# Gated products of three token tiles and the sample moved from ahead of the first expert tile into its stream of slots

## The chip, the cores and the metric

The program runs on one core of a Trainium2 chip (trn2). The metric is the device time of one execution in microseconds. A core has five engines that run their own instruction lists and meet at semaphores: TensorE (PE in the profile, its weight loads PEld), VectorE (DVE), ScalarE (ACT), GpSimd (POOL) and SyncE (SP); 16 DMA engines move data between memory (HBM), the on-chip buffer (here one tensor, `arena`, 53200 floats on each of 128 partitions) and itself. SP, ACT and POOL issue transfers.

## The reference

One step of a two-layer trunk, in float32, for a prompt of 512 tokens and a sample of 8 rows, with width 1024. Layer 0 is a state-space mixer, then an expert layer; layer 1 is latent attention, then an expert layer; every part has a modulated norm before it and a gated sum after it. The parts that the change touches:

```python
y = jnp.real(jnp.einsum("blgn,gpn->blgp", h, c_mat)) + d_skip * uf      # state-space output
z = jax.nn.gelu(y.reshape(bsz, length, D_MODEL))
a, g = jnp.split(z @ w_glu, 2, axis=-1)                                  # w_glu: 1024 x 2048
out = a * jax.nn.sigmoid(g)                                              # the gated product
x = x + ga1 * out
h = modulate(rmsnorm(x, g_norm[layer, 1]), sh2, sc2)
# experts: q = h @ w_q (1024 x 2048), scores against 2 x 128 keys for each of 8 heads,
# the best 16 of 16 x 16 candidates of each head, g = softmax of their scores; then for each of
# the 128 chosen experts of a token:  act = gelu(h . u[idx]);  y += g * act * v[idx]
x = x + ga2 * peer(h, w_q, sub_keys, u_emb, v_emb)
```

## The kernel before

**The gated product** (TensorE from L2080, ScalarE from L1062, VectorE from L1556, SP from L690). When the last round `y` of the state products is copied out, ScalarE applies the gelu in five instructions (four quarters j of the prompt and the sample) to `z5`. Here "j" isn't a run of 128 tokens: a chunk holds eight tokens, 2 halves of 4, and j is the place in the half, so the result has to go through memory (`x1_dram`) to come back as tiles of 128 consecutive tokens. For each j TensorE turns the 8 blocks (L2089), ScalarE copies them (L1069), and then come four units: unit q is the product with one quarter of the columns of `w_glu`, arranged so that a unit holds 256 columns of a and the 256 of g that belong to them, 8 matmuls of 128x512 (L2101). Two banks of PSUM alternate. ScalarE makes the sigmoid of g (L1077), VectorE multiplies (L1562), and after four units multiplies by the gate of the modulation and adds the residual row (L1568). SP stores each j (L704), waits for all stores, and only then issues the loads of the expert layer: modulation rows, the first two tiles (L744), and the query weights in four quarters (L730) and the keys.

**The expert layer** works on tiles t of 128 tokens (0 to 3 in layer 0; tile 4 is the sample). What each engine does in which order is written out by `peer_plan`: a list of steps that every engine goes through, doing the steps that are its own. The preparation of a tile is: squares, means, roots, norm, shifted (a modulated norm), turn, turned, then four query quarters m of four pieces each (`query`, L2132, eight 128x128 matmuls a piece), with a copy (L1107), a score product (`score`, L2145) and its copy (L1116) after each. Then for each of 8 heads six steps `top` (VectorE's search for the best 16, which writes the head's 16 row numbers) and shift, exps, gates (the softmax). The stream of a tile is 128 slots. In slot m GpSimd gathers one row of u and v for each token (L938, 1 MiB in one indirect DMA) into one of six ring buffers; VectorE makes the dot (L1688); ScalarE a gelu, a product with the gate and a diagonal of 32x32 blocks (L1146, L1158, L1161); TensorE adds the weighted v to the sum in PSUM (L2185, eight matmuls on 32x32 blocks). GpSimd reuses a ring buffer after TensorE's sum. The preparation of tile t+1 is spread over the slots of tile t by the lists `extra[slot]`; for tile 0 it stands ahead of the first slot as far as its first head, and heads 1 to 7 are done in slots 1 to 45, six steps a head.

Sigmoid, exp, sqrt and gelu need different tables in ScalarE, so a change between them shows as ACT_TABLE_LOAD.

Of the kernel before, what the change touches and what calls it, by code (L numbers as in the profile page):

```python
# [11 lines left out]
ALU = mybir.AluOpType  # L12
# [3 lines left out]
P = 128  # L16
# [4 lines left out]
NB = 8  # L21
# [37 lines left out]
def program(nc, a):  # L59

    with ExitStack() as ctx:
# [84 lines left out]
        z5 = at(SJ, (TC // 2) * D).rearrange("p (j d) -> p j d", j=TC // 2)  # L146
# [71 lines left out]
        s_x1 = sem("mixer_out_ready")  # L218
        s_out = sem("outputs_stored")
# [7 lines left out]
        LATE_GLU, LATE_Q, LATE_HEADS = 16, (48, 128), 96  # L227
# [7 lines left out]
        def row_no(passes, stage, j):  # L235

            slot = row_slot(stage, j)
            before = sum(row_slot(q, m) == slot for q in passes[:passes.index(stage)] for m in range(5))
            return 16 * (before + sum(row_slot(stage, m) == slot for m in range(j + 1)))
# [33 lines left out]
        zt = [at(U2 + i * D, D).rearrange("p (k t) -> p k t", k=KD) for i in range(2)]  # L273
        gate = [at(U2 + 2 * D + i * 256, 256) for i in range(2)]
        glu_t = [at(U2 + 2 * D + 512 + i * D, D) for i in range(2)]
        QW = KD * MB
        wglu_at = [at(MINB, QW)] + [at(CL + q * QW, QW) for q in range(3)]
# [33 lines left out]

        def rows_of(t):
            return P if t % 5 < 4 else NB
# [24 lines left out]
        s_pmr = sem("peer_mods_ready")  # L338
# [37 lines left out]
        def peer_plan(layer):  # L376
# [26 lines left out]
            for steps in first[:21]:  # L403
                plan += steps
            plan += [("top", t0, 0, part) for part in range(6)]
            plan += [("shift", t0, 0, 1), ("exps", t0, 0, 1), ("gates", t0, 0, 1)]
            for b in range(5):
                t = t0 + b
                extra = [[] for _ in range(slots_of(t))]
                if b == 0:  # L410
                    for m, steps in enumerate(first[21:36]):
                        extra[m // 3] += steps
                    for h in range(1, PH):
                        for part in range(6):
                            extra[6 * h + part - 5].append(("top", t0, h, part))
                        extra[6 * h].append(("shift", t0, h, h + 1))
                        extra[6 * h + 1].append(("exps", t0, h, h + 1))
                        extra[6 * h + 2].append(("gates", t0, h, h + 1))
# [31 lines left out]
        EXPS = [step for plan in PLAN for step in plan if step[0] == "exps"]  # L450

        def exp_no(t, h0):

            return [step[1:3] for step in EXPS].index((t, h0)) + 1

# [161 lines left out]
        def _(sp):  # L617
# [65 lines left out]
            sp.dma_start(wglu_at[0], a["w_glu"][:, 0:QW]).then_inc(s_wglu, 16)  # L683
# [6 lines left out]
            wait_copied(sp, ("y", NR - 1))  # L690
            sp.wait_ge(s_wglu, 16)
            for q in range(1, 4):
                sp.dma_start(wglu_at[q], a["w_glu"][:, QW * q:QW * (q + 1)]).then_inc(s_lw if q == 1 else s_wglu, 16)
            sp.wait_ge(s_out, 32)
            for s in range(2):
                sp.dma_start(at(BL, 4 * D, 64 * s, 64 * s + 64), x5v[s]).then_inc(s_x5, 16)
            sp.dma_start(at(BL + 4 * D, D, 0, NB), a["x_sample"]).then_inc(s_x5, 16)
            sp.dma_start(at(BL + 5 * D, D, 0, NB), mod_dram[1:NC9, 2 * D:3 * D]).then_inc(s_x5, 16)
            sp.dma_start(mod_a, mod_dram[0:1, 2 * D:3 * D].partition_broadcast(P)).then_inc(s_x5, 16)
            x1v = x1_dram.rearrange("(c s j) d -> s j c d", s=2, j=TC // 2)  # L700
            for j in range(TC // 2):
                sp.wait_ge(s_x1, j + 1)
                for s in range(2):
# [1843 lines left out]
```

## Time and profile before

| | us |
|---|---|
| median of 3 runs (lowest, highest) | 3956.45 (3954.03, 3964.04) |
| the profiled execution | 3956.18 |
| its span, first to last instruction | 3954.4 |
| mean granted TensorE clock in it | 0.761 of full speed |

| engine | busy us in the span | share |
|---|---|---|
| PE | 2770.6 | 70% |
| DVE | 2377.8 | 60% |
| ACT | 1232.7 | 31% |
| POOL | 1197.0 | 30% |

The page cuts the span into 40 slices of 98.9 us. Each digit is the share of the slice in which the engine was busy, in tenths, and 9 means 90% or more. Line numbers (L2101) are those of the kernel. In a group of instructions "out<-in" names the tensors, the shape stands as partitions x elements, and a float32 matmul leaves two records, so that a unit of eight matmuls is x16. In brackets stands the idle time of the engine before the instruction and what ended it.

### The profile page before, as it was taken

The numbers are of one execution on the slowest core, as the hardware profiler recorded it, in microseconds if no ns is written. First come the engines' busy times: TensorE is split into PE (matmuls) and PEld (weight loads), VectorE is DVE, ScalarE is ACT, GpSimd is POOL, SyncE is SP. The second block draws the span as 40 slices with busy tenths as digits, with TensorE's granted clock in tenths as the row PEclk, the third lists the DMA queues.
The fourth block names the chain that finished last, engine by engine and source line by source line (L and its number), as shares of the span: only waits on it lengthen the run. The fifth ranks groups of instructions, "written<-read, shape, count | busy, mean of one in ns | idle before, by whom it ended". The sixth has DMA issues, their size and how long they took to land.

```text
span 3954.4 us, 63127 instructions
## 1 busy us (share of the span) xinstructions
PE 2770.6 (70%) x24972; PEld 1044.8 (26%) x24972; DVE 2377.8 (60%) x5650; ACT 1232.7 (31%) x3821; POOL 1197.0 (30%) x1089
## 2 busy tenths in 40 slices
PE   4565877776866866656677899677768668766665
PEld 2354333320400410100043566442204003100100
DVE  8544018787677677554522344277886766775645
ACT  1212004433333333323321222134343334334333
POOL 5200003344444444433300001033444444443432
PEclk7767987777967866757788899777768677776767
DMA  8764238999999999999920203479999999999997
GB/s 325 182 190 134 78 139 323 387 409 420 409 420 420 415 416 419 418 405 419 381 67 6 94 17 150 161 306 392 407 420 401 420 420 412 412 420 401 417 421 329
DMA packets 208878, 1263.84 MB, mean 320 GB/s; under 512 B 54488, under 2 KB 55392, under 8 KB 62520
## 3 DMA queue, kind: packets, MB, share of 16 engines
q0 software_dynamic: 151552, 1109.46, 68.6%
q1 hardware_dynamic: 56480, 150.09, 11.2%
q8 instruction: 181, 2.97, 0.3%
q10 hardware_dynamic: 576, 0.59, 0.0%
q14 instruction: 89, 0.73, 0.0%
HBM read 1247.58 MB, written 10.12 MB: 318 GB/s over the span
## 4 chain that ended last, share of the span: by engine, by line
DMA 40%; PE 32%; DVE 17%; ACT 5%; issue 4%; SPq 1%; DVEq 1%; POOL 0%; ACTq 0%; PEldq 0%; POOLq 0%
DMA arena<-peer_uv,arena 35%; PE psum L2185 9%; DVE arena L1688 8%; PE psum L2132 6%; PE psum L2101 3%; DMA arena<-b_mod 2%; PE psum L2460 2%; PE psum L2263 2%; PE psum L2236 1%; DVE arena L1599 1%; ACT arena L1161 1%; ACT arena L1158 1%; ACT arena L1146 1%; PE psum L2324 1%; DVE arena L1351 1%
## 5 line engine op out<-in xcount | busy, mean ns | idle before, releaser
L2185 PE MATMUL psum<-arena 32*32 32x512 f32 x16384 | 1583.2, 848 | 813.9 <-ACT arena L1161 810.0
L1688 DVE SCALAR_TENSOR_TENSOR arena<-arena 128x1024 f32<-128x1024 f32 x1040 | 1274.8, 1226 | 784.7 <-DMA arena<-peer_uv,arena 773.8
L938 POOL DMA_INDIRECT arena<-peer_uv,arena x1040 | 1095.1, 1053 | 2148.8 <-PE psum L2185 1525.4
L2185 PEld LDWEIGHTS psum<-arena 32*32 32x32 f32 x16384 | 219.2, 121 | 2065.7 <-ACT arena L1161 2015.5
L1146 ACT ACTIVATE arena<-arena 128x1 f32<-128x1 f32 x1040 | 210.5, 202 | 1561.0 <-DVE arena L1688 1560.4
L1161 ACT ACTIVATE arena<-arena 128x32 f32<-128x32 f32 x1024 | 329.0, 321 | 33.4
L1158 ACT ACTIVATE arena<-arena 128x1 f32<-128x1 f32 x1040 | 306.0, 294 | 33.8
L2132 PE MATMUL psum<-arena 128*128 128x128 f32 x2048 | 269.3, 289 | 7.3 <-DMA arena<-peer_wq 6.2
L2132 PEld LDWEIGHTS psum<-arena 128*128 128x128 f32 x2048 | 251.4, 201 | 80.7 <-issue 79.2
L1342 DVE TENSOR_TENSOR arena<-arena 128x512 f32<-128x512 f32 (+6 forms) x187 | 156.0, 834 | 95.2 <-ACT arena L1252 76.8
L2020 PE MATMUL psum<-arena 128*9 128x128 f32 x2048 | 100.4, 377 | 111.3 <-DMA arena<-b_mod 111.3
L2101 PE MATMUL psum<-arena 128*128 128x512 f32 (+1 forms) x320 | 142.7, 607 | 17.1 <-DVE arena L1562 10.7
L2020 PEld LDWEIGHTS psum<-arena 128*9 128x9 f32 x2048 | 71.5, 122 | 138.8 <-issue 100.0
L1562 DVE TENSOR_TENSOR arena<-psum,arena 128x256 f32<-128x256 f32 (+1 forms) x20 | 8.4, 422 | 148.7 <-ACT arena L1077 116.9
L1351 DVE SCALAR_TENSOR_TENSOR arena<-arena 128x1024 f32<-128x1024 f32 (+3 forms) x61 | 70.9, 1163 | 40.7 <-DMA arena<-mod_rows 22.0
L1010 ACT ACTIVATE arena<-psum 9x128 f32<-9x128 f32 x128 | 34.5, 269 | 193.5 <-PE psum L2025 191.1
L970 POOL DMA_INDIRECT arena<-cache_kv,arena x8 | 7.5, 942 | 267.6 <-PE psum L2346 206.1
L1599 DVE MAX8 arena<-arena 128x8 f32<-128x128 f32 (+1 forms) x204 | 61.9, 331 | 43.9 <-ACT arena L1116 41.5
L1688 DVE DVE_READ_ACCUMULATOR arena<-arena 128x1 f32 x1040 | 85.5, 82 | 0.0
L2101 PEld LDWEIGHTS psum<-arena 128*128 128x128 f32 (+1 forms) x320 | 55.3, 175 | 101.5 <-issue 93.8
L1883 DVE TENSOR_REDUCE arena<-psum 128x1 f32<-128x128 f32 (+3 forms) x64 | 31.4, 490 | 84.2 <-PE psum L2327 83.8
L2460 PE MATMUL psum<-arena 128*128 128x512 f32 (+1 forms) x160 | 77.7, 648 | 4.8 <-ACT arena L1312 4.8
(262 smaller groups left out, 2503.8 us busy)
## 6 DMA issues: line engine op xcount, KB each, us to landing
arena<-w_mod SPq DMA_DIRECT2D x64, 1024.0 KB
arena<-peer_uv,arena POOLq DMA_INDIRECT x1040, 10.4
arena<-peer_wq SPq DMA_DIRECT2D x8, 2048.0 KB, 16.7
arena<-w_glu SPq DMA_DIRECT2D x4, 2048.0 KB, 12.4
arena<-x_prompt SPq DMA_DIRECT2D x4, 1024.0 KB
arena<-x_after_layer SPq DMA_DIRECT2D x8, 512.0 KB
arena<-w_o SPq DMA_DIRECT2D x1, 4096.0 KB
arena<-mod_rows SPq DMA_DIRECT2D x2, 1536.0 KB
```

Of the source, the lines that this page charges most:

```text
L938: pool.indirect_dma_start(ring[r], None, a[f"peer_uv{t // 5}"], bass.IndirectOffsetOnAxis(ap=ix, axis=0)).then_inc(landed[r], 16)
L1146: act.activation(col, col, ACT.Gelu_apprx_tanh).then_inc(s_gl, 1)
L1158: act.activation(wcol, col, ACT.Copy, scale=gate_).then_inc(s_gl, 1)
L1161: act.activation(diag[:, n_ % RING, :], eye32, ACT.Copy, scale=wcol).then_inc(s_dg, 1)
L1342: link(dve.tensor_tensor(out, x, y, op))
L1351: link(dve.scalar_tensor_tensor(out=out, in0=x, scalar=s, in1=y, op0=op0, op1=op1))
L1688: dve.scalar_tensor_tensor(out=u, in0=u, scalar=1.0, in1=h, op0=ALU.mult, op1=ALU.mult, accum_out=at(DOTS + (t % 2) * 2 * P + m, 1)).then_ ...
L2020: ins = pe.matmul(mod_bank(b, q), silu[:, k, :], w[k // 4][:, k % 4, MQ4 * q:MQ4 * (q + 1)], start=(k == 0), stop=False, skip_group_check= ...
L2101: ins = pe.matmul(psum[0:rows, 4 + m % 2, :], zt[j % 2][:, k, 0:rows], wglu[:, k, :], start=(k == 0), stop=(k == KD - 1))
L2132: ins = pe.matmul(psum[:, 4 + m % 2, P * q:P * q + R], wq[:, m, k, P * q:P * (q + 1)], htr[:, k, 0:R], start=(k == 0), stop=(k == KD - 1))
L2185: ins = pe.matmul(acc_of(t, i, c), diag[rows, r, :], ring[r][rows, D + 512 * c:D + 512 * (c + 1)], start=(m == 0), stop=last, skip_group_c ...
L2460: ins = pe.matmul(psum[0:R, 6 + n_, :], ot[:, k, 0:R], wo[:, k, 512 * n_:512 * (n_ + 1)], start=(k == 0), stop=(k == KD - 1))
```

## The change

Tokens are now taken in runs of 128: the copy of the turned blocks puts them in order of tokens (`ztv`), so that the residual row is a plain tile of `x_prompt`, and the sum stays where the expert layer reads it. All 32 turns of the prompt are done at once, the gelus go by rounds, and only the four units of tokens 0 to 127 stand ahead of the expert layer. The 12 units of tokens 128 to 511 and one unit of the sample (four products side by side in four column strips) are steps `glu` of the plan in slots 4 to 55 of tile 0, a quarter of a unit in each, with `gate` (sigmoid) one slot and `gsum` (VectorE's three steps on 256 columns) two slots after a unit's last quarter. To give the weights of the gated product a place, the query weights of tile 0 are loaded into the ring buffers and one more place (`WQ0`), and loaded again into their own place as the quarters of `w_glu` are done with (`glu_beside_experts`); quarter 0 of `w_glu` is loaded twice too. GpSimd's first six gathers therefore wait for query products. Two more query quarters stand ahead of the first slot (`ahead = 26`), the heads 2 to 7 of tile 0 are spread over slots 7 to 60, tile 1's preparation begins at slot 58 instead of 40, and two of its heads are searched in its own stream. Only tiles 2 and 3 and the sample are stored to `x1_dram`.

```diff
             first = [[] for _ in range(64)]
             prep(t0, first, 0)
-            for steps in first[:21]:
+            ahead = 21 if layer else 26
+            for steps in first[:ahead]:
                 plan += steps
...
                         for part in range(6):
-                            extra[6 * h + part - 5].append(("top", t0, h, part))
-                        extra[6 * h].append(("shift", t0, h, h + 1))
...
+                            m = 6 * (h - 1) + part
+                            m = 1 + m if layer or m < 6 else 7 + int(1.5 * (m - 6))
+                            extra[m].append(("top", t0, h, part))
...
+                    if layer == 0:
+                        for u in range(4, len(UNITS)):
+                            m = 4 * (u - 3)
+                            for piece in range(4):
+                                extra[m + piece].append(("glu", u, piece))
+                            extra[m + 4].append(("gate", u))
+                            extra[m + 5].append(("gsum", u))
+                        extra[100].append(("smods",))
+                if t == 1:
+                    for m in range(12):
+                        extra[1 + int(1.3 * m)].append(("top", t, 6 + m // 6, m % 6))
...
-                    at_ = 40 if b == 0 else 10
+                    at_ = 58 if t == 0 else 40 if b == 0 else 10
                     prep(t + 1, extra, at_)
                     at_ += 22 if b < 3 else 30
-                    gap = 1.3 if b == 0 else 1.5 if b == 3 else 1.75
-                    heads = heads_of(t + 1)
+                    gap = 1.25 if t == 0 else 1.3 if b == 0 else 1.5 if b == 3 else 1.75
+                    heads = 6 if t == 0 else heads_of(t + 1)
...
+            sp.wait_ge(s_mm, len(ROUNDS))
+            for q in (1, 2):
+                sp.dma_start(at(WGLU[q], QW), a["w_glu"][:, QW * q:QW * (q + 1)]
+                             ).then_inc(s_lw if q == 1 else s_wglu, 16)
+            sp.dma_start(at(X1[0], D), a["x_prompt"][0:P]).then_inc(s_x5, 16)
...
+            sp.dma_start(at(WGLU[3], QW), a["w_glu"][:, QW * 3:QW * 4]).then_inc(s_wglu, 16)
+            sp.wait_ge(s_out, 32)
+            sp.dma_start(at(KEYS, 2 * PH * P), a["peer_keys"][0]).then_inc(s_pw, 16)
+            for m in range(4):
+                if m == 0:
+                    sp.wait_ge(s_zt, 4)
+                if m == 1:
+                    sp.wait_ge(s_gm, 2)
+                sp.dma_start(at(WQ0[m], QW), a["peer_wq"][0][:, QW * m:QW * (m + 1)]
+                             ).then_inc(s_lw if m else s_pw, 16)
...
+            sp.wait_ge(s_pq, 4)
+            sp.dma_start(at(WGLU[0], QW), a["w_glu"][:, 0:QW]).then_inc(s_wglu, 16)
+
+            def glu_beside_experts():
+
+                for m, q in enumerate((1, 2, 3, 0)):
+                    sp.wait_ge(s_gm, units_done(q))
+                    peer_weights(0, m)
...
+                for j in (2, 3):
+                    sp.wait_ge(s_x1, x1_no(j))
+                    sp.dma_start(x1_dram[P * j:P * (j + 1)], at(X1[j], D)).then_inc(s_out, 16)
...
                 if n_ >= RING:
                     pool.wait_ge(freed[r], n_ // RING)
+                else:
+                    pool.wait_ge(s_pq, n_ // 2 + 1)
...
+            for r in range(NR):
+                wait_copied(act, ("y", r))
+                act.activation(z5[:, :, RG * GP * r:RG * GP * (r + 1)].rearrange("p j (g q) -> p j g q", g=RG),
+                               h5[:, RG * r:RG * (r + 1)].rearrange("p g j q -> p j g q"), ACT.Gelu_apprx_tanh
+                               ).then_inc(s_gelu, 1)
...
+            def glu_gate(u):
+
+                act.wait_ge(s_gm, u + 1)
+                if u >= 2:
+                    act.wait_ge(s_ga, u - 1)
+                act.activation(gate[u % 2], psum[:, unit_bank(u), 256:512], ACT.Sigmoid).then_inc(s_sg, 1)
...
+                if t == 1:
+                    dve.wait_ge(s_out, 32 + 48)
...
+                n_ = KD // pieces
+                for k in range(n_ * piece, n_ * (piece + 1)):
+                    if j == 4:
+                        for c in range(4):
+                            ins = pe.matmul(psum[32 * c:32 * c + NB, unit_bank(u), :], zts[:, k, :],
+                                            wide(WGLU[c])[:, k, :], start=(k == 0), stop=(k == KD - 1))
+                    else:
+                        w = wide(WGLU0 if u == 0 else WGLU[q])
+                        ins = pe.matmul(psum[:, unit_bank(u), :], ztk[:, k, P * j:P * (j + 1)], w[:, k, :],
+                                        start=(k == 0), stop=(k == KD - 1))
```

## Rows read from the trace of the kernel before

**Rows 1.** The page's slices, 98.9 us each: GB/s moved by the DMA engines.

```profile
GB/s 325 182 190 134 78 139 323 387 409 420 409 420 420 415 416 419 418 405 419 381 67 6 94 17 150 161 306 392 407 420 401 420 420 412 412 420 401 417 421 329
```

**Rows 2.** Stretches: length, busy us and instructions of each engine, clock, DMA share, GB/s.

```profile
395.00:410.00 15.00, 15.00 (x32) 6.23 (x31) 0.00 (x0) 1.22 (x2) 0.00 (x0) 0.90 1.03 355
...
421.00:555.00 134.00, 130.21 (x320) 52.08 (x320) 17.19 (x26) 9.88 (x22) 0.00 (x0) 0.98 0.07 16
...
640.00:744.00 104.00, 64.96 (x640) 9.13 (x640) 98.56 (x302) 53.35 (x144) 39.15 (x38) 0.66 0.99 395
744.00:832.00 88.00, 75.58 (x832) 42.74 (x824) 58.97 (x155) 31.24 (x105) 36.85 (x34) 0.90 0.99 391
```

**Rows 3.** Waits from 380 to 613 us: total us, times, longest.

```profile
ACT arena L1077 <- PE psum L2101: 146.8, 20, 19.6
```

**Rows 4.** Instructions in order of time, gated products to first gather: start, us.

```profile
394.59 15.74 PE L2101 MATMUL psum<-arena 128*128 128x512 f32 x32 [2.80 <-ACT arena L1069]
...
410.37 0.38 ACT L1077 ACTIVATE arena<-psum 128x256 f32<-128x256 f32 x1 [6.48 <-PE psum L2101]
...
421.02 16.16 PE L2101 MATMUL psum<-arena 128*128 128x512 f32 x32 [10.70 <-DVE arena L1562]
...
430.77 0.42 DVE L1562 TENSOR_TENSOR arena<-psum,arena 128x256 f32<-128x256 f32 x1 [9.56 <-ACT arena L1077]
...
498.61 27.73 PE L2101 MATMUL psum<-arena 128*128 128x512 f32 x64 [1.11 <-ACT arena L1069]
...
558.26 0.28 SPq L706 DMA_DIRECT2D xs_after_mixer<-arena  x1
...
570.50 1.03 ACT L1085 ACTIVATE psum<-arena 128x1024 f32<-128x1024 f32 x1 [15.21 <-DMA arena<-x_after_mixer]
...
584.16 13.39 PE L2132 MATMUL psum<-arena 128*128 128x128 f32 x96 [6.20 <-DMA arena<-peer_wq]
...
608.04 1.11 POOL L938 DMA_INDIRECT arena<-peer_uv,arena  x1 [437.86 <-DVE arena L1654]
```

**Rows 5.** Instructions in order of time, in the stream of slots.

```profile
613.67 1.23 DVE L1688 SCALAR_TENSOR_TENSOR arena<-arena 128x1024 f32<-128x1024 f32 x1 [4.66 <-DMA arena<-peer_uv,arena]
...
636.40 1.28 ACT L1138 ACT_TABLE_LOAD   x1
...
637.93 1.28 ACT L1146 ACT_TABLE_LOAD   x1
...
639.48 1.23 DVE L1688 SCALAR_TENSOR_TENSOR arena<-arena 128x1024 f32<-128x1024 f32 x1
...
655.72 1.22 DVE L1688 SCALAR_TENSOR_TENSOR arena<-arena 128x1024 f32<-128x1024 f32 x1
...
770.42 2.05 PE L2132 MATMUL psum<-arena 128*128 128x128 f32 x16
772.40 1.09 PE L2185 MATMUL psum<-arena 32*32 32x512 f32 x16
...
784.17 2.05 PE L2132 MATMUL psum<-arena 128*128 128x128 f32 x16
...
952.24 1.23 DVE L1688 SCALAR_TENSOR_TENSOR arena<-arena 128x1024 f32<-128x1024 f32 x1 [1.25 <-DMA arena<-peer_uv,arena]
...
1661.82 1.05 PE L2153 MATMUL psum<-arena 128*8 128x512 f32 x8
```

**Rows 6.** Fourth tile beside loads: gather landings 640 to 744, then 1697 to 1750.

```profile
DMA to landing us min/median/max: 7.5/9.0/10.5
...
DMA to landing us min/median/max: 15.4/20.7/27.3
...
L1688 DVE SCALAR_TENSOR_TENSOR arena<-arena x25: 1224/1226/1227, 1684.6 to 1772.0; 128x1024 f32<-128x1024 f32 x25
...
1691.73 1.96 PE L2185 MATMUL psum<-arena 32*32 32x512 f32 x16 [1.39 <-ACT arena L1161]
...
arena<-w_uq SPq DMA_DIRECT2D x1, 3072.0 KB
```

More of the change, by code:

```diff
@@ L237, in row_no @@
             slot = row_slot(stage, j)
-            before = sum(row_slot(q, m) == slot for q in passes[:passes.index(stage)] for m in range(5))
-            return 16 * (before + sum(row_slot(stage, m) == slot for m in range(j + 1)))
+            mine = [(q, m) for q in passes[:passes.index(stage) + 1] for m in range(5 if q != stage else j + 1)
+                    if row_slot(q, m) == slot and not (passes is LOADS and q == "peer0" and m < 2)]
+            return 16 * len(mine)
         ROUNDS = ([("u", r) for r in range(NR)] + [("k", r) for r in range(NR)]
@@ L410, in peer_plan @@
                 if b == 0:
-                    for m, steps in enumerate(first[21:36]):
+                    for m, steps in enumerate(first[ahead:36]):
                         extra[m // 3] += steps
@@ L1202, in peer_act @@
                         final_roots(*which)
+                    elif what == "gate":
+                        glu_gate(*which)
             def input_squares(j):
@@ new lines, in peer_mods, with glu_sum @@
+            def peer_mods(layer, rows, gain):
+                sc = at(PMOD + (D if rows == P else 4 * D), D, 0, rows)
+                return dve.scalar_tensor_tensor(out=sc, in0=sc, scalar=1.0, in1=at(gain, D, 0, rows), op0=ALU.add,
+                                                op1=ALU.mult)
+            dve.wait_ge(s_pmod, 32)
+            link(peer_mods(0, P, PTMP))
+            dve.wait_ge(s_x5, 48 + 32)
+            def glu_sum(u):
+                j, q = UNITS[u]
+                if u == 4:
+                    dve.wait_ge(s_x1r, 16 * 5)
+                dve.wait_ge(s_sg, u + 1)
+                quarters = range(4) if j == 4 else (q,)
+                for c in quarters:
+                    rows = slice(0, P) if j < 4 else slice(32 * c, 32 * c + NB)
+                    y = glut if j < 4 else at(GLUT, 256, 0, NB)
+                    ga = at((GA if j < 4 else GAS) + 256 * c, 256, 0, P if j < 4 else NB)
+                    x = at(X1[j] + 256 * c, 256) if j < 4 else at(X1S + 256 * c, 256, 0, NB)
+                    ins = dve.tensor_tensor(y, psum[rows, unit_bank(u), 0:256], gate[u % 2][rows], ALU.mult)
+                    if c == quarters[-1]:
+                        ins.then_inc(s_ga, 1)
+                        dve.wait_ge(s_ga, u + 1)
+                    else:
+                        link(ins)
+                    tt(y, y, ga, ALU.mult)
+                    ins = dve.tensor_tensor(x, x, y, ALU.add)
+                    if c == quarters[-1] and (j == 4 or (j, q) == [unit for unit in UNITS if unit[0] == j][-1]):
+                        ins.then_inc(s_x1, 1)
+                        dve.wait_ge(s_x1, x1_no(j))
+                    else:
+                        link(ins)
@@ L1572, in peer_means, with sample_mods @@
+            for u in range(4):
+                glu_sum(u)
+            def sample_mods():
+                dve.wait_ge(s_pmod, 80)
+                link(peer_mods(0, NB, HSP))
             def peer_means(t):
@@ L2200, in peer_pe @@
                         peer_turn(*which)
+                    elif what == "glu":
+                        glu_piece(*which)
                     elif what == "query":
```

241 lines of the change are left out of this document (130 added, 111 removed).

## The prediction

> **What bounds the kernel now.** I read the page's slices first: 78 and 139 GB/s are moved in the fifth and sixth slice (395 to 593 us), and 387 to 420 from the eighth on, up to the attention part [rows 1]. The table of stretches says why: from 421 to 555 us TensorE is busy 130 of 134 us at nearly full clock while 16 GB/s move; from 640 us on the transfers hold 391 to 395 GB/s at a share of 0.99 and TensorE has idle time in most of it [rows 2]. The first is the gated product, 20 units of eight 128x512 products (4 tiles and the sample times 4 weight quarters). The second is the expert stream: each slot gathers 1 MiB (1.049 MB, 2.50 us at the 420 GB/s of the fuller slices), VectorE forms a dot, ScalarE a weight, TensorE a weighted sum. The waits ahead of the stream say the same: ScalarE waits 146.8 us for the products of L2101, once for each of 20 units [rows 3]. What is done there for tiles 1 to 3 and the sample isn't needed by the first expert tile, and GpSimd issues nothing until 608.04 us [rows 4].
>
> The stream of the first tile isn't purely DMA-bound. Its 128 slots run from 613.67 to 952.24 us, 338.6 us or 2.65 each [rows 5]. In slots 8 to 47 VectorE is full: six slots take 16.24 us (2.71 each), which hold six dots and one head's search [rows 5], and it is busy 98.56 of 104 us [rows 2]. In the stretch with the next tile's queries TensorE sets the pace: a query piece of 2.05 and a sum of 1.09, overlapping a little, in four slots of five; five slots take 13.75 us, 2.75 each [rows 5].
>
> **The start of the stream, step by step.** (a) Today the first product starts at 394.59 us [rows 4]. After the change the gelus go round by round beside the state products, so only the last is left behind them, but all 32 turns and four copies come before the first product. Today one gelu of the five, eight turns and one copy lie there, after one gelu of four everything else is ready; I estimate +0.9 us, within -1 and +4. (b) Four units remain: the first two as now, 15.74 us, two more at 6.87 (four take 27.73) = 13.7, then gate 0.38 and three 256-wide VectorE steps of 0.42 with gaps, 1.9 [rows 4]. They end at 426.9 us. The stall of 10.70 us in front of the third unit [rows 4], where VectorE waits for the last row load, goes: the four units have a bank each and the gate row is loaded earlier. Late next are the weights: the third unit needs 8 MiB (8.4 MB) that start at 386 us, 24 us at the 355 GB/s of that stretch today [rows 2], 410 against the unit's 411; it is hidden with nothing to spare, which is most of the +4. (c) The way through memory, from 558.26 (store) to 570.50 (squares), 12.24 us, goes, since the row is left in the tile. (d) From the squares to the first gather is 37.54 us; in it TensorE idles 6.20 us until 584.16 for query weights, of which a copy of the turned rows needs about 1.1 (the squares over as many elements took 1.03) [rows 4]. Those weights are now issued beside the units (11 MiB, 32 us at 355 GB/s, by 418 us), so 32.5 stay. The order ahead of the stream holds one or two more query quarters, but they run beside VectorE's search and delay only what no one waits for; GpSimd's new wait for a query count in its first six gathers is met before each is due. First gather: 394.59+0.9+31.4+32.5 = 459.4 us instead of 608.0. Gain 148.6 us, bounds 144 to 151.
>
> **What the stream pays back.** Twelve prompt units and the sample unit stand in slots 4 to 56, a quarter each.
> TensorE: a quarter is two 128x512 products, 1.73 us at 27.73/32 each; with the sum, about 1.04 of its 1.09 in sequence, 2.77 per slot. The sample piece is four products in four column strips; the sample query of that form takes 1.05 us a step [rows 5], two steps 2.1, so it is no worse.
> VectorE: 13 sums of products (three steps of 0.42 and gaps, 1.4; the sample's four times that) and the sample's modulation of 1.2, 23.6 us, against two heads' searches moved to the next tile (2 x 9.3 from 16.24 less six dots of 1.15, 18.7). In slots 7 to 60 the searches are spread 1.5 times wider: per nine slots 10.4 + 9.3 + 3.2 = 22.9, 2.54 per slot. It stops being the bound.
> ScalarE: 13 sigmoids of 0.38 and two table loads each of 1.28 [rows 5], 38 us, in an engine busy about half of the time [rows 2].
> DMA: the query weights are loaded a second time into their own place (8 MiB), one gated quarter a second time (2), rows stored (1) and broadcast (0.5): 11.5 MiB, 28.7 us at 420 GB/s, where there was room of 338.6 - 319.6 = 19 us. By slot 56 some 8 of them share with 53 gathers: 2.88 per slot.
> So three engines stand at 2.5 to 2.9 and share a ring of six. How bursts of loads act on such a ring is seen in the fourth tile: 9.2 MiB of attention weights (w_uq's 3 are shown) come in at 1697 us, gathers land in 20.7 us instead of 9.0, and the 24 slots from 1684.6 take 87.4 us instead of 59.9, 27.5 more or 3.0 per MiB [rows 6].
> That is the share one expects from the Trainium skill, "DMA: Bandwidth & Descriptors", section on queues, rings and completion order: each engine goes round its queue rows packet by packet, so issue from another engine buys no extra rate. By that rule, the trace agrees: the loads take about half.
> I take 3.0 per slot in slots 4 to 56. Sum for the first tile: 4 slots at 3.2 = 13; 53 at 3.0 = 159; 12 at 2.5 with 3.5 MiB of loads and stores = 39; 21 with queries at 2.75 = 58; 38 at 2.5 = 95; together 364, 25 more than 338.6. From below, transfers alone need 348.3 (+10). From above, every MiB costs 3.0 on top of today's pace (+35). Second tile: two heads' searches in slots 1 to 17, where VectorE already reads sums; 3 us, 0 to 6.
>
> Net: 148.6 - 25 - 3 = 120.6 us. Against the profiled execution's 3956.18 us: 3835.6; its time is within 0.3 us of the median, so I say 3836.
>
> **Waits added, and who stands behind them.** ScalarE's gate waits for TensorE's unit, and behind it stand the next slots' weights; VectorE's sum waits for the gate, and behind it stand the dots. Both are only tied to TensorE within two slots, less than the ring's six. SP waits for units before it loads over their weights; behind it stand the stores of tiles 2 and 3, and for those VectorE waits before it normalises tile 1 (slot 61). That is five slots after the last unit, behind 3 MiB on a shared path, 15 us against about as much time: 0 to 5 us, inside the bounds.
>
> **Rivals.** A (forecast): 3815 to 3858. B, the stream hides nearly all: transfers alone bound it, 3956.2 - 151 + 10 = 3815, or 3812 with tile 2's share at its lowest; for it speaks that TensorE's part in slots 4 to 56 is just 2.77, against it that bursts cost 3.0 per MiB where they were seen. C, the gates sit on the path: each of 13 units makes sum, gate and table loads serial, 13 x (1.28+1.28+0.38) = 38 us more, 3874; for it: the switch at 636.40 is followed by the next at 637.93, and all weights stand behind them [rows 5]; against it: TensorE has 2.7 us of its own to do after the unit, and ScalarE's idle time covers it.
> The Trainium skill, "ScalarE: Activation LUTs", on what a table load costs, puts a drain of about 1.38 us on each load of 1.283. By it C would be 13 x (2 x 2.66 + 0.38) = 74, 3910. The trace disagrees with the drain: the second load starts 1.53 us after the first, with an exponential between them.
> D, slower than before: TensorE stays at its 1.2 GHz level from the first unit to slot 56. A sum then takes 1.96 [rows 6] and a gated piece twice 1.73; 5.4 per slot instead of 3.0 for 53 slots is 127 us more, and four units at half speed another 25: 3988. It decides from the point where four fifths of that time (120.6 of 152 us) are at that level. For it: the granted clock is 0.66 from 640 to 744 us, so the engine falls back there. Against: wherever long products stand in the stream or fill the engine it is 0.90 to 0.98 [rows 2]. E, it doesn't do what it says: the first gather still comes after 560 us because something waits for a late unit or load; I find no such wait in the diff. It would give about 3940.
>
> **How the numbers follow.** A 0.60, B 0.12, C 0.13, D 0.03, E 0.02, other stalls in the stream beyond C 0.10. Predicted is A's 3836. The range must reach to B's 3812 and most of the way into C: 3872. A measurement tells about 0.3% (12 us) from no change. Faster by more: A, B, C and most of the rest, 0.95; within it 0.02; slower 0.03.
>
> **What would show it.** First gather at 456 to 464 us; no wait of ScalarE on the row's load; 32 turns before four units, which end near 427. First tile's dots 350 to 375 us from first to 129th; slots 4 to 56 near 3.0 with a granted clock of 0.9 or more and TensorE busy nearly throughout; 11.5 MiB more on the hardware queue after the first gather; landings longer than 10 us while weights come. Everything after the second tile should be moved as it stands. Wrong would be: slots 4 to 56 above 3.4, a gather start above 470, or a difference in the second layer.

## The result, and the profile after

The changed kernel takes 3841.35 us (median of 4 runs, 3840.18 to 3844.84) against 3959.53 us of the kernel before in the same comparison: a ratio of 0.9705, 95% interval 0.9693 to 0.9717, or 118 us less. The forecast was 3836. The profiled execution took 3840.18 us, its span 3838.4.

The slices of the page, 96 us each, answer to [rows 1]: the two starved slices (78 and 139 GB/s) are gone, and a full one comes from the sixth slice on.

```profile
GB/s 328 190 163 158 279 388 399 407 413 407 420 420 414 408 420 420 421 402 421 187 13 85 23 61 179 174 385 382 417 420 407 419 418 405 420 420 400 417 421 327
```

The way to the first gather, from the timeline (start, us, engine, line; it answers to [rows 4]; L2235 is the gated product, L1151 its gate, L1167 the squares, L1012 the gather, which were L2101, L1077, L1085 and L938):

```profile
396.01 29.43 PE L2235 MATMUL psum<-arena 128*128 128x512 f32 x64 [2.08 <-DVE arena L1639]
...
427.34 1.03 ACT L1167 ACTIVATE psum<-arena 128x1024 f32<-128x1024 f32 x1 [1.05 <-DVE arena L1671]
...
435.92 13.74 PE L2274 MATMUL psum<-arena 128*128 128x128 f32 x96 [1.11 <-ACT arena L1181]
...
460.15 1.11 POOL L1012 DMA_INDIRECT arena<-peer_uv,arena  x1 [289.58 <-DVE arena L1770]
...
465.86 1.23 DVE L1804 SCALAR_TENSOR_TENSOR arena<-arena 128x1024 f32<-128x1024 f32 x1 [4.50 <-DMA arena<-peer_uv,arena]
...
831.46 1.23 DVE L1804 SCALAR_TENSOR_TENSOR arena<-arena 128x1024 f32<-128x1024 f32 x1 [1.25 <-DMA arena<-peer_uv,arena]
```

Four units run back to back with no stall before the third, nothing goes through memory, and the queries no longer wait for weights. The waits ahead of the stream answer to [rows 3]: four units instead of twenty (total us, times, longest).

```profile
ACT arena L1151 <- PE psum L2235: 28.3, 4, 8.8
```

The stream pays back. Stretches of it (length, busy us of TensorE, its weight loads, VectorE, ScalarE and GpSimd, clock, share of the transfers, GB/s; they answer to [rows 2]):

```profile
460.00:490.00 30.00, 24.02 (x216) 14.40 (x219) 18.24 (x63) 10.04 (x29) 12.83 (x12) 1.00 0.94 386
490.00:640.00 150.00, 142.49 (x1026) 40.26 (x1027) 126.13 (x362) 92.11 (x201) 49.68 (x49) 1.00 0.99 393
640.00:670.00 30.00, 12.22 (x124) 1.94 (x130) 16.09 (x35) 13.13 (x32) 7.34 (x8) 0.67 1.01 388
```

From 490 to 640 us TensorE is busy 142 of 150 us. The share of the transfers, 0.99, looks like a second full resource, but a share alone doesn't show a limit: in the same kernel it is 1.01 at 420 GB/s from 540 to 550 us and still 0.86 at 289 GB/s from 550 to 560. Whether the transfers hold the stream is seen in who waits for them. The waits from 490 to 640 us (total us, times, longest; L1012 is the gather, L2327 TensorE's sum, L1664 VectorE's first step of a gated product, L1791 a step of the softmax, L1804 the dot):

```profile
POOL arena L1012 <- PE psum L2327: 100.5, 49, 4.2
DVE arena L1664 <- ACT arena L1151: 10.4, 7, 2.3
DVE arena L1791 <- ACT arena L1220: 6.4, 5, 1.3
DVE arena L1804 <- DMA arena<-peer_uv,arena: 2.0, 1, 2.0
```

GpSimd waits for TensorE's sums before nearly every gather, and of some 50 dots only one waits for its rows, for 2.0 us. It starts at 615.79 us, just behind a 2 MiB load of query weights. One slot, from TensorE's timeline (it answers to the pieces in [rows 5]):

```profile
578.87 1.09 PE L2327 MATMUL psum<-arena 32*32 32x512 f32 x16
579.89 1.98 PE L2235 MATMUL psum<-arena 128*128 128x512 f32 x4
581.80 1.09 PE L2327 MATMUL psum<-arena 32*32 32x512 f32 x16
```

A sum and a quarter of a unit take 2.93 us (581.80 - 578.87): 1.02 to the piece's start and 1.91 for the piece. And one new wait, on VectorE, between the dots of slots 60 and 61:

```profile
663.20 0.16 DVE L1703 RECIPROCAL arena<-arena 128x1 f32<-128x1 f32 x1 [9.95 <-DMA x_after_mixer<-arena]
```

First-tile dots, read from the timeline of VectorE, in the forecast's own pieces:

| slots | before, us | forecast | after |
|---|---|---|---|
| 0 to 4 | 10.4 | 13 | 13.3 |
| 4 to 57 | 145.3 | 159 | 164.0 |
| 57 to 69 | 32.6 | 39 | 38.8 |
| 69 to 90 | 55.1 | 58 | 53.8 |
| 90 to 128 | 95.2 | 95 | 95.6 |
| first tile | 338.6 | 364 | 365.6 |
| second tile | 325.2 | 328 | 329.7 |
| third and fourth | 675.4 | 675.4 | 674.3 |

### The profile page after: what moved, and what is told of

It is laid out like the page before. It is cut to its first block, busy times and chain, and to the rows that moved or that the text cites. A ratio compares the mean times of both kernels' runs of the same rounds, so it can differ in the third digit from the quotient of the medians.

```text
span 3838.4 us, 63188 instructions
## 1 busy us (share of the span) xinstructions
PE 2733.9 (71%) x24972; PEld 1028.6 (27%) x24972; DVE 2386.7 (62%) x5687; ACT 1265.4 (33%) x3843; POOL 1204.8 (31%) x1089
## 4 chain that ended last, share of the span: by engine, by line
DMA 39%; PE 32%; DVE 17%; ACT 6%; issue 4%; SPq 1%; DVEq 1%; POOL 0%; ACTq 0%; PEldq 0%; POOLq 0%
DMA arena<-peer_uv,arena 35%; PE psum L2327 10%; DVE arena L1804 7%; PE psum L2274 6%; DMA arena<-b_mod 2%; PE psum L2604 2%; PE psum L2235 2%; PE psum L2407 2%; PE psum L2380 1%; ACT arena L1241 1%; ACT arena L1238 1%; DVE arena L1715 1%; ACT arena L1228 1%; DVE arena L1433 1%; PE psum L2468 1%
## 5 line engine op out<-in xcount | busy, mean ns | idle before, releaser
L2327 PE MATMUL psum<-arena 32*32 32x512 f32 x16384 | 1570.0, 841 | 771.2 <-ACT arena L1241 758.1
L1804 DVE SCALAR_TENSOR_TENSOR arena<-arena 128x1024 f32<-128x1024 f32 x1040 | 1273.5, 1226 | 766.9 <-DMA arena<-peer_uv,arena 751.9
L1012 POOL DMA_INDIRECT arena<-peer_uv,arena x1040 | 1102.8, 1060 | 2025.8 <-PE psum L2327 1561.0
L2327 PEld LDWEIGHTS psum<-arena 32*32 32x32 f32 x16384 | 218.5, 120 | 2006.5 <-ACT arena L1241 1917.6
L1238 ACT ACTIVATE arena<-arena 128x1 f32<-128x1 f32 x1040 | 306.0, 294 | 33.8
L1424 DVE TENSOR_TENSOR arena<-arena 128x512 f32<-128x512 f32 (+7 forms) x202 | 158.4, 784 | 93.1 <-ACT arena L1334 73.7
L2235 PE MATMUL psum<-arena 128*128 128x512 f32 x256 | 124.7, 619 | 2.1 <-DVE arena L1639 2.1
L1804 DVE DVE_READ_ACCUMULATOR arena<-arena 128x1 f32 x1040 | 85.3, 82 | 0.0
L2604 PE MATMUL psum<-arena 128*128 128x512 f32 (+1 forms) x160 | 77.7, 648 | 4.8 <-ACT arena L1394 4.8
L1366 ACT ACTIVATE arena<-psum,arena 128x128 f32<-128x128 f32 (+3 forms) x64 | 33.8, 528 | 128.5 <-DVE arena L1996 128.5
```

The source lines that it names most:

```text
L1012: pool.indirect_dma_start(ring[r], None, a[f"peer_uv{t // 5}"], bass.IndirectOffsetOnAxis(ap=ix, axis=0)).then_inc(landed[r], 16)
L1238: act.activation(wcol, col, ACT.Copy, scale=gate_).then_inc(s_gl, 1)
L1424: link(dve.tensor_tensor(out, x, y, op))
L1804: dve.scalar_tensor_tensor(out=u, in0=u, scalar=1.0, in1=h, op0=ALU.mult, op1=ALU.mult, accum_out=at(DOTS + (t % 2) * 2 * P + m, 1)).then_ ...
L2235: ins = pe.matmul(psum[:, unit_bank(u), :], ztk[:, k, P * j:P * (j + 1)], w[:, k, :], start=(k == 0), stop=(k == KD - 1))
L2327: ins = pe.matmul(acc_of(t, i, c), diag[rows, r, :], ring[r][rows, D + 512 * c:D + 512 * (c + 1)], start=(m == 0), stop=last, skip_group_c ...
```

## The experiments

The question to settle was: what holds slots 8 to 55 at 3.03 us? The forecast put 3.0 down to bursts of loads on the transfers; the trace shows TensorE at 2.93 as well. So I took the second load of weights, half of TensorE's products and ScalarE's table switches away one at a time, then in pairs and all three, and tried versions that spread the work. "Pace" is the mean of one slot over slots 8 to 55. All are medians, and each ratio is to the kernel before, run on the same chip.

| kernel | us (runs' range) | ratio, 95% interval | pace, us | first tile, us |
|---|---|---|---|---|
| changed | 3841.35 (3840.18 to 3844.84) | 0.9705 (0.9693 to 0.9717) | 3.029 | 365.6 |
| a_again2 | 3842.05 (3838.67 to 3849.95) | 0.9707 (0.9690 to 0.9724) | 3.043 | 369.0 |
| v_stores_first | 3838.48 (3830.07 to 3842.62) | 0.9709 (0.9696 to 0.9723) | 3.050 | 365.0 |
| v_spread | 3836.57 (3835.70 to 3844.01) | 0.9708 (0.9695 to 0.9721) | 3.036 | 369.2 |
| v_small_loads | 3841.34 (3839.63 to 3843.11) | 0.9699 (0.9686 to 0.9712) | 3.005 | 365.9 |
| e_small_loads_only | 3849.48 (3846.95 to 3855.26) | 0.9717 (0.9704 to 0.9731) | 3.050 | 374.4 |
| e_late_queries | 3842.54 (3841.95 to 3844.21) | 0.9701 (0.9684 to 0.9718) | 3.070 | 371.0 |
| e_no_reload2 | 3835.10 (3831.16 to 3837.25) | 0.9680 (0.9664 to 0.9696) | 3.016 | 363.3 |
| e_same_table2 | 3839.51 (3836.79 to 3848.12) | 0.9700 (0.9683 to 0.9718) | 3.012 | 367.2 |
| e_half_products2 | 3842.66 (3840.48 to 3844.84) | 0.9704 (0.9688 to 0.9720) | 3.021 | 365.9 |
| e_no_reload_table | 3835.17 (3824.67 to 3836.47) | 0.9674 (0.9652 to 0.9695) | 2.964 | 358.6 |
| e_half_no_reload | 3823.19 (3819.98 to 3831.77) | 0.9660 (0.9638 to 0.9681) | 2.846 | 352.2 |
| e_all_three | 3819.51 (3818.05 to 3820.95) | 0.9642 (0.9625 to 0.9659) | 2.774 | 347.5 |

### The changed kernel again, and the stores first

The changed kernel itself, as the measure for the others:

> The changed kernel once more, as the yardstick on the same chip. Both theories: 3841 us within 0.2%, a first gather near 460 us, slots 8 to 55 of the first tile at 3.03 us each, 365.6 us from the first dot to the 129th.

Two profiled executions of it differ by 0.014 us in the pace and 3.4 us in the first tile. The profile of e_late_queries, whose slots are the same, lies further off (3.070 and 371.0 us; its granted clock is 0.91 from 480 to 500 us, where the changed kernel has 1.00). A difference under 0.04 us in the pace or 5.4 us in the first tile therefore shows nothing by itself.

In the first version the stores of tiles 2 and 3 go ahead of the last load of query weights, so that VectorE's wait of 9.95 us should go.

```
                 for m, q in enumerate((1, 2, 3, 0)):
+                    if m == 3:
+                        for j in (2, 3):
+                            sp.wait_ge(s_x1, x1_no(j))
+                            sp.dma_start(x1_dram[P * j:P * (j + 1)], ...
```

> The stores of tiles 2 and 3 are issued before the last load of query weights instead of behind it. The 10.0 us for which VectorE waits for them at tile 1's norm should fall under 3. If the stream is not bound by transfers there, 6 to 9 us less than the changed kernel, 3833; if the transfers that the stall lets through had to be made anyway, 0 to 3 us less, 3839. I expect 4 less, 3837.

The wait for the stores is gone, as expected, but the 4 us are not: slots 56 to 64 take 28.9 us against 31.1 and 29.6 in the two profiles of the changed kernel, and neither the first tile (365.0) nor the whole can be told from it. From 640 to 680 us VectorE now waits for gathers, 13.3 us in nine waits, where the changed kernel has 10.0 us for the stores and 6.5 for gathers. So the wait was mostly the place where a backlog showed: the bytes have to be moved in either order.

### One suspect at a time

e_no_reload2 leaves out nearly all of the second load of the query weights, so other experts are chosen for tiles 1 to 3 and the sample:

```
-                    peer_weights(0, m)
+                    sp.dma_start(at(WQ + m * QW, 64), a["peer_wq"][0][:, m * QW:m * QW + 64])...
```

> Leaves out most of the second load of the first layer's query weights (8 MiB become 128 KB), so the choice of experts of tiles 1 to 4 is another one; the number of gathers and of all other instructions stays. Theory P (TensorE sets slots 4 to 55: 1.91 us for a quarter unit and 1.02 for the sum, 2.93 per slot): slots 8 to 55 stay at 3.03 within 0.05; only what comes after slot 56 is shorter, 2 MiB and part of the 10 us wait for the stores, in all 6 to 10 us, 3833. Theory M (the prediction's: transfers in bursts make the 3.0): slots 8 to 55 fall to 2.77 to 2.85, 9 to 12 us more, 3822.

```profile
490.00:640.00 150.00, 141.93 (x1024) 39.95 (x1024) 124.82 (x352) 91.32 (x201) 50.09 (x49) 1.00 0.95 355
```

The rate falls from 393 to 355 GB/s, no dot in slots 8 to 55 waits for its rows, and the pace stays (3.016): TensorE holds it, still busy 142 of 150 us. Slots 57 to 69 take 33.8 us instead of 37.4, about half of the 7 us by which the whole is shorter than a_again2.

e_half_products2 leaves out every second product of the prompt's units in the stream:

```
+                    if pieces == 4 and j < 4:
+                        if k % 2 == 0:
+                            ins = pe.matmul(psum[:, unit_bank(u), :], ztk[:, k, ...], ...
```

> Leaves out every second of the eight products of the 12 prompt units in the stream, so these sums are over half of the contraction. TensorE then needs about 1.0 + 1.0 = 2.0 us per slot. Theory P: slots 8 to 55 fall from 3.03 to the next limit, 2.6 (VectorE) to 2.9 (gathers and 6 to 8 MiB of loads), 8 to 18 us less, 3823 to 3833. Theory M: transfers are the limit already, less than 5 us, 3836 or more.

```profile
490.00:640.00 150.00, 115.88 (x954) 25.04 (x954) 126.07 (x358) 92.46 (x204) 53.83 (x50) 0.93 0.98 394
```

TensorE drops to 116 of 150 us, and the pace stays too (3.021). I had expected 8 to 18 us from it. Theory M, which expected under 5 us, had the number right, but the transfers are not a limit in every slot. The waits of the same stretch show the chain:

```profile
PE psum L2331 <- ACT arena L1241: 33.6, 23, 3.3
ACT arena L1228 <- DVE arena L1804: 47.5, 34, 4.6
DVE arena L1804 <- DMA arena<-peer_uv,arena: 7.2, 3, 3.1
```

TensorE (its sum is L2331 here) waits for ScalarE's weight, ScalarE for VectorE's dot, and VectorE for a gather only three times. All three fall beside a 2 MiB load or within 3 us of its end: those that end at 573.65 and 577.99 us (the load's packets run from 567.6 to 576.8) and at 613.25 (602.9 to 610.5). With TensorE out of the way, VectorE's own list and these late landings hold the stream. TensorE's gain is also smaller than its work: the clock granted to it is 0.93 here, where the changed kernel has 1.00.

e_same_table2 puts a gelu in the place of the sigmoid in the stream, so that no table is switched for it:

```
-                act.activation(gate[u % 2], psum[:, unit_bank(u), 256:512], ACT.Sigmoid)
+                act.activation(gate[u % 2], psum[:, unit_bank(u), 256:512],
+                               ACT.Sigmoid if u < 4 else ACT.Gelu_apprx_tanh)
```

> The 13 gates in the stream use the gelu instead of the sigmoid, another function of the same cost, so that ScalarE loads no table for them; the residual rows differ. Theory P: ScalarE's two loads per unit lie beside TensorE's work; only TensorE's short waits for a diagonal go, 0 to 8 us, 3833 to 3841. Theory C (gates on the path, 2.56 us for each of 13 units): 33 us less, 3808.

ScalarE's busy time from 490 to 640 us falls from 92.11 to 59.23 us, and the time by nothing that can be told. Rival C of the prediction, which priced these loads at 38 us, is not what happens.

### Two at a time, and three

The products halved and the second load left out, the two edits above together:

> Both at once: half the products of the 12 prompt units in the stream left out, and the second load of the query weights cut to 128 KB. Alone each left slots 8 to 55 at 3.02. Theory J (two limits stand at the same height, TensorE at 2.93 and transfers with their bursts at about 2.9): together the slots fall to what VectorE and ScalarE need, 2.60 to 2.75, 13 to 20 us less in those slots, 3818 to 3826 in all. Theory R (one other thing, the order of steps or the gates, sets 3.0): they stay at 2.95 or more.

```profile
490.00:640.00 150.00, 113.89 (x982) 24.01 (x982) 131.64 (x371) 96.93 (x217) 54.00 (x52) 0.94 0.96 373
```

The pace falls to 2.846 and the time by 19 us against a_again2, though one part alone gave nothing and the other 7. That is what two limits of nearly the same height do. The slot stayed above the 2.60 to 2.75 that I expected. What the second limit is, VectorE's time over slots 8 to 55 shows (us; each stretch ends at the dot of slot 56):

| kernel | length | VectorE busy | waits for gathers | for the gates | for the exponentials |
|---|---|---|---|---|---|
| changed | 145.4 | 121.9 | 2.0 | 10.4 | 6.4 |
| e_no_reload2 | 144.8 | 121.8 | 0 | 11.9 | 6.4 |
| e_half_products2 | 145.0 | 121.7 | 7.2 | 5.4 | 6.1 |
| e_half_no_reload | 136.6 | 121.7 | 0 | 4.3 | 6.0 |
| e_all_three | 133.1 | 121.4 | 0.9 | 0.8 | 5.3 |

VectorE's work is the same in all of them, 2.54 us a slot. With all products, TensorE's late units make it wait for the gates; with half of them it waits as much, now for gathers that land late beside a load. Only with both gone is the stream shorter, by 8.4 us, of which the waits for gathers are 7.2. So the second limit is VectorE's list together with the bursts of loads.

The second load left out and no table switched:

> The second load of the query weights cut to 128 KB and the 13 gates with the gelu, so that no table is loaded for them; all products are made. Theory J: TensorE alone is left as a limit, its waits for ScalarE go: slots 8 to 55 at 2.93 to 2.96. If ScalarE's loads were a limit of their own beside TensorE: under 2.9, which TensorE's own 2.93 excludes.

A slot takes 2.964 us and the first tile 358.6, and between 550 and 640 us TensorE is busy throughout: with the loads gone, the switches show a little, down to nearly TensorE's 2.93. The gain over e_no_reload2, 0.05 us a slot, is hardly more than profiles of the same slots differ by, and the whole takes the same time (3835.17 and 3835.10 us).

> Half products, no second load, no table loads for gates. Theory J: 2.55 to 2.65 per slot in slots 8 to 55, which is VectorE's 2.54 or the gathers' 2.50 with little lost. If the table loads cost something once the other limits are gone, it is the difference to the kernel without the first two alone: 0 to 5 us.

```profile
490.00:640.00 150.00, 113.90 (x1012) 23.93 (x996) 132.97 (x370) 66.44 (x193) 61.72 (x53) 0.93 0.98 384
```

Here the three edits stand together. A slot takes 2.774 us, not the expected 2.55 to 2.65, and the whole 3819.51 us. The stretch shown reaches 22 us past slot 56; in slots 8 to 55 VectorE is busy 121.4 of 133.1 us and waits 0.9 us for gathers and 0.8 for gates (the table above). So VectorE's list is the next limit, not the transfers with their share of 0.97 there: it needs 2.53 us a slot, and the 0.24 us on top are 0.11 of waits for ScalarE's exponentials, 0.04 of those two and short gaps.

### Spreading the work, and smaller loads

v_spread puts the quarters into slots 4 to 64 instead of 4 to 56, and moves a head's search to the next tile; the stores go first:

```
-                            m = 4 * (u - 3)
+                                m = 4 + int(1.18 * (4 * (u - 4) + piece))
...
-                    at_ = 58 if t == 0 else 40 if b == 0 else 10
+                    at_ = 67 if t == 0 else 40 if b == 0 else 10
```

> Stores first, and the 52 quarters spread over slots 4 to 64 instead of 4 to 55, tile 1's preparation from slot 67 instead of 58, three of its heads in its own stream instead of two. Theory P: TensorE needs 1.02 + 1.91/1.18 = 2.64 per slot, so slots 8 to 64 come down to what transfers need, about 2.85, first tile 355 us instead of 366; 3830. Theory M: no better than stores first alone.

TensorE goes from 142 to 134 of 150 us, and the pace remains 3.036. The expectation was wrong: I had lowered one of two equal limits. VectorE's waits for gathers grow from 2.0 to 9.7 us in the stretch, the longest 5.4 us behind a 2 MiB load. The two small-load kernels then cut each second load of 2 MiB into four of 512 KB, three slots apart, on top of v_spread and alone (the pieces of the last load go two slots apart in v_small_loads and at once in e_small_loads_only, whose lines are shown):

```
-                    peer_weights(0, m)
+                    for i in range(4):
+                        if i and m < 3:
+                            sp.wait_ge(s_dots, QUARTER_SLOT[m] + 3 * i)
+                        sp.dma_start(at(WQ + m * QW + i * QW // 4, QW // 4), ...
```

> v_spread with each second load of the query weights (2 MiB) cut into four of 512 KB, issued three slots apart, so that no 2 MiB piece stands in the queue ahead of gathers or stores. It computes everything. Theory J (what holds the slots at 3.0 us beside TensorE is the burst of a 2 MiB load, during which the gathers' landings are late; v_spread has already lowered TensorE's share of a slot): slots 8 to 55 at about 2.85 us, tile 0 about 358 us, the whole about 3830 us. Rival (the mean rate of all transfers, or the order of the steps in VectorE's stream, sets 3.0 us and the size of a piece changes nothing): slots at 3.03 us, tile 0 at 367 us, 3836 us.

> The changed kernel with the three second loads of the query weights before the last cut into four of 512 KB, three slots apart, and nothing else but the last load's split into four issued at once. It computes everything. Theory of two limits side by side (TensorE with 2.93 us a slot stays): slots 8 to 55 at 3.00 us, give or take 0.03, the whole 0 to 3 us under the changed kernel, about 3840 us. Rival (the bursts alone made 3.03 us of 2.93): slots at 2.95 us, the whole about 3837 us.

v_small_loads: 3.005 and 3841.34 us. From 490 to 640 us:

```profile
490.00:640.00 150.00, 135.81 (x1019) 37.44 (x1017) 126.59 (x359) 87.50 (x201) 56.37 (x51) 0.97 0.99 393
```

TensorE and the bursts are both eased, and the expected 10 us don't come. VectorE's waits for gathers do fall, from 9.7 us in v_spread to 3.9, the longest from 5.4 to 1.2, but its waits for gates rise from 5.4 to 9.2 (from 490 to 640 us). The pace is 0.03 us lower, which is within what profiles of the same slots differ by. The bytes moved in the stretch, 393 GB/s, don't decide between the mean rate and the bursts: nearly the same bytes at nearly the same pace give the same rate, whatever holds the pace. The rival's 3.03 and 367 us are nearer than theory J's numbers, but what it says of the size of a piece isn't borne out by the waits. e_small_loads_only came out worse than either expectation. The last pieces are issued later, the stores behind them on SP at 645.58 us instead of 641.78, and VectorE waits longer in the same place:

```profile
670.33 0.16 DVE L1710 RECIPROCAL arena<-arena 128x1 f32<-128x1 f32 x1 [14.86 <-DMA x_after_mixer<-arena]
```

That is 4.9 us of the 8.8 by which its first tile is longer.

### The early query weights

e_late_queries issues the weights of the first queries after the fourth unit instead of beside them:

```
-                if m == 1:
-                    sp.wait_ge(s_gm, 2)
+                    sp.wait_ge(s_gm, 4)
```

> The first layer's query weights for the first tile are issued only after its four gated units, as late as they were before the change relative to the squares, but without the modulation rows, keys and rows in front of them. The prediction priced their early issue at 5.1 us. If a 2 MiB load on an idle path lands in 7 us, it comes before its use at 435.9 us, and the first gather moves by less than 1 us, 3841; by the prediction's step it moves by up to 5.

```profile
418.16 1.84 SPq L760 DMA_DIRECT2D arena<-peer_wq  x4
...
441.52 3.81 PE L2273 MATMUL psum<-arena 128*128 128x128 f32 x32 [3.55 <-DMA arena<-peer_wq]
...
455.81 1.12 POOL L1011 DMA_INDIRECT arena<-peer_uv,arena  x1 [290.02 <-DVE arena L1769]
```

The units end at 418.0 us here and at 425.4 in the changed kernel. The part ahead of them varies from run to run, and the units themselves take 27.8 us here and 29.4 there, at a granted clock of 1.00 against 0.89 from 395 to 410 us. So the step is read from their end: 37.8 us to the first gather against 34.8. The overlap of these weights is worth 3.0 us on this path, more than the under 1 expected; the whole time doesn't tell it.

## Why the prediction came out as it did

**Start of the stream.** Forecast 459.4 us, measured 460.15. (a) First product 395.5, measured 396.01. (b) Four units and their sums by 426.9; the squares start at 427.34. The stall before the third unit is gone, and no unit waited for weights. (c) The way through memory is gone. (d) 32.5 us from the squares to the gather; 32.81. The gain is 147.9 us of 148.6. This worked because each term was a row of the trace before, and the path after it was the same instructions.

**The first tile.** Forecast 25 us longer, measured 27.0 (and 30.4 in a_again2). The sum was right to 1.6 us, with these terms off or right for another reason:
- Slots 4 to 57: 159, measured 164.0. TensorE's quarter was mis-sized: it went in at 1.73 us, taken from long runs of such products, and takes 1.91 between two sums. That makes 2.93 per slot, not 2.77. In the 145.4 us of slots 8 to 55 TensorE is busy 138.0 us and waits for ScalarE's weights in the rest. The 3.0 of the forecast came from elsewhere, from bursts of loads: 8 MiB of them were to lift the slots above the 2.88 of the transfers. Here they cost little, because TensorE was as late (VectorE waits 2.0 us for gathers); they cost 7.2 us where TensorE has half its products. So the mechanism exists, but it was not what set the pace, and that 3.0 was near was luck in part.
- The 2.88 per slot at 420 GB/s can't be judged by the 393 GB/s of the stretch. The same 61 MiB (64.0 MB) over 53 slots make 3.07 us at 393, but the rate is the bytes over the pace, whatever sets the pace. The 395 GB/s of [rows 2] was no ceiling either: VectorE was busy 98.56 of 104 us there.
- VectorE: 2.54 per slot forecast, 2.54 us busy measured. But "it stops being the bound" counted only its work. With its waits for gates and exponentials and its gaps it doesn't come under 2.77 in any run, so it stood close behind TensorE.
- VectorE's wait for the stores: 0 to 5 us, measured 9.95. The place and the reason were right (stores behind 2 MiB of query weights); the load landed later than assumed. The ring filled meanwhile, and slots 61 to 64 took 4.9 us; slots 57 to 69 sum to 38.8 us against the forecast 39, which is luck in part.
- Slots 69 to 90: 58, measured 53.8, but 58.1 in a_again2, so the two profiles don't tell whether the term was off. [rows 5]'s five-slot stretch at 2.75 was not the mean of it before (55.1 us, 2.62 a slot).

**Later tiles.** Two moved searches at the head of the second tile: 3 forecast, 4.5 measured (325.2 to 329.7). a_again2 has 327.6 us, so the term holds as far as two profiles tell. The third and fourth tile: no change forecast, 1.1 us less measured.

**The sum.** 147.9 - 27.0 - 4.5 + 1.1 - 0.1 (from the gather to the first dot) = 117.4 us up to the end of the fourth tile. The two profiled executions differ by 116.0 us (3956.18 - 3840.18), against the forecast 120.6. The rest of the program differs by about 1 us, no more than runs do. Of the 5.4 us between 3841.35 and 3836, 0.7 are the head, 2.0 the first tile and 1.5 the second, less 1.1 in the third and fourth; the rest lies behind the fourth tile and between the profiled execution and the median, and is no more than runs differ by.

**Rivals.** B, transfers alone bound it at 3812: TensorE stands at 2.93, and VectorE's list at 2.77. Even with all three edits the time is 3819.51. C, switches on the path at 38 us: false by e_same_table2. Gates do make VectorE wait, 10.4 us in slots 8 to 55; 6.9 us of it stay without the table loads, and 5.4 with half the products. ScalarE loads the sigmoid's table before it waits for the unit, then the gelu's table, and the gelu of an expert weight follows at once:

```profile
580.13 1.28 ACT L1151 ACT_TABLE_LOAD   x1
581.91 0.38 ACT L1151 ACTIVATE arena<-psum 128x256 f32<-128x256 f32 x1 [0.50 <-PE psum L2235]
582.31 1.28 ACT L1228 ACT_TABLE_LOAD   x1
583.61 0.20 ACT L1228 ACTIVATE arena<-arena 128x1 f32<-128x1 f32 x1
```

Four of these steps stand within 3.7 us. The Trainium skill, "ScalarE: Activation LUTs", on what a table load costs, adds a drain of about 1.38 us to each; the trace disagrees here too, since the load at 582.31 starts 0.02 us after the sigmoid's end, and the next activation 0.02 us after the load. D, TensorE at its 1.2 GHz level: false, the granted clock is 1.00 from 460 to 640 us, where the engine had long products in every slot. Its mean falls to 0.67 in 640 to 670 us, after the last quarter, when TensorE is busy 12.22 of 30 us with sums alone. E, something holds the first gather back: false, it comes at 460.15 us.

**What stays open.** Why a quarter of a unit takes 0.18 us more between sums than in a long run, and why VectorE has 4.6 to 4.7 us of short gaps in 48 slots in every kernel of the table above. The share of time in slots 8 to 55 that TensorE's limit and VectorE's each hold can't be split either: the stream passes from one to the other.

## What to carry to other kernels

Work moved under a stream is paid by the resources that the stream has already filled. Price a short piece of work by rows where it stands between other shapes. Don't take a share of 0.99, or the rate beside it, for a limit: the rate is the bytes over the pace. Look at who waits for a landing, and how long. Add an engine's waits to its work before you say that it stops being the bound. When two limits stand at nearly the same height, take away both in one experiment before you judge either: alone they gave 7 and 0 us, together 19. A long wait in the trace can be just the place where a backlog becomes visible; moving its stores forward gave nothing that could be measured.

## What the runs showed of the hardware

- Two 128x512 fp32 products take 1.91 us from start to start between groups of 32x32 sums (579.89 to 581.80), where a long run of such products has 0.87 us each (27.73 us for 32 before): some 0.18 us more each time. Of the quarters from 490 to 640 us that are followed by a sum without a wait, all 38 take 1.91 or 1.92 us.
- The share of the transfers is no rate and no limit. It is 1.01 at 420 GB/s (540 to 550 us of the changed kernel), 0.99 at 393 (490 to 640 us), 0.86 at 289 (550 to 560 us), and 0.97 at 385 in slots 8 to 55 of e_all_three, where VectorE waits 0.9 us for gathers.
- While a load runs beside the gathers, the two queues take turns by packets, so the queue with the larger packets gets more of the bytes. First the changed kernel from 608 to 615 us, beside a 2 MiB load, then v_small_loads from 605 to 609 us, beside one of 512 KB (q1 has SP's loads and q0 the gathers; packets, MB, share of 16 engines):

```profile
q1 hardware_dynamic: 126, 2.06, 69.1%
q0 software_dynamic: 131, 0.95, 32.9%
...
q0 software_dynamic: 166, 1.22, 73.9%
q1 hardware_dynamic: 127, 0.44, 27.2%
```

  A packet of the 2 MiB load has 16 KB on the mean, one of the smaller load 3.5 KB and one of the gathers 7.3 KB. The gathers get 136 GB/s beside the 2 MiB load and 305 GB/s beside the smaller one. The Trainium skill, "DMA: Bandwidth & Descriptors", section on queues, rings and completion order, has each engine take turns between its queue rows packet by packet. The trace agrees with it in the first stretch, 126 packets against 131; in the second it is 127 against 166. In the prediction's own case, the kernel before from 1710 to 1720 us, the loads have 160 packets of 319 but 3.15 of 4.31 MB, so "about half" holds for packets there and not for bytes.
